# Output projections in four column quarters, with expert weights loaded during them

## What is computed

```
layer 0:  z = [attention(8 heads x 64), HGRN2 recurrence(8 heads x 64)]    # 544 x 1024
          h = h + z @ w_out_ab                                            # output projection 0
          h = h + moe(rmsnorm(h))
layer 1:  bg, cg, hh = split(rmsnorm(h) @ w_in_c)                         # 3 x 1024 columns
          g = bg * conv3(cg * hh)                                         # short convolution
          h = h + g @ w_out_c                                             # output projection 1
          h = h + moe(rmsnorm(h))
moe:      each frame takes its best of 4 groups and in it its best 2 of 8 experts;
          out = sum over both of  gate * (silu(x @ w1[e]) * (x @ w3[e])) @ w2[e]
```

## Time and profile before

| | us |
|---|---|
| median of 3 runs (1251.95 to 1252.97) | 1252.25 |
| profiled execution | 1252.11 |
| its span | 1250.4 |
| TensorE busy in it | 1019.9 (82%) |
| VectorE busy | 437.0 (35%) |
| ScalarE busy | 276.9 (22%) |
| GpSimd busy | 197.7 (16%) |
| moved by DMA | 282.56 MB, mean 226 GB/s |

### The profile page before, as it was taken

One profiled execution on the slowest core, in us unless ns is written; L12 is line 12 of the kernel. 1 busy time (PEld: TensorE's weight loads), 2 busy tenths in 40 slices (PEclk: granted clock), 3 DMA queues, 4 the chain that ended last, 5 costly groups with the idle time before them and its releaser, 6 DMA issues.

```text
span 1250.4 us, 17904 instructions
## 1 busy us (share of the span) xinstructions
PE 1019.9 (82%) x7539; PEld 766.2 (61%) x7539; DVE 437.0 (35%) x894; ACT 276.9 (22%) x538; POOL 197.7 (16%) x139
## 2 busy tenths in 40 slices
PE   5989999879789569987788259999995699777781
PEld 4988999754467345544444159999874455444440
DVE  5333574547823511101100466545435211110114
ACT  4244322125501111111111331221112112111110
POOL 3343431004210012211111000000000122111110
PEclk9999999767889769998888669999997699888996
DMA  6322221404002989999998822233228899999975
GB/s 209 89 68 77 93 81 37 109 9 153 2 6 101 373 308 413 415 417 416 416 416 336 256 70 75 76 101 117 1 101 336 333 412 415 416 417 415 417 313 223
DMA packets 110686, 282.56 MB, mean 226 GB/s; under 512 B 22890, under 2 KB 61846, under 8 KB 94196
## 3 DMA queue, kind: packets, MB, share of 16 engines
q1 hardware_dynamic: 100884, 263.66, 56.3%
q0 software_dynamic: 9728, 17.85, 3.8%
HBM read 270.57 MB, written 27.02 MB: 238 GB/s over the span
## 4 chain that ended last, share of the span: by engine, by line
PE 59%; DMA 22%; DVE 8%; SPq 5%; ACT 2%; issue 2%; POOL 1%; DVEq 0%; POOLq 0%; ACTq 0%
DMA w<-in_w_dram 16%; PE banks L981 12%; PE banks L902 11%; PE banks L846 9%; PE banks L621 8%; PE banks L913 4%; SPq L377 3%; PE banks L620 3%; DMA wab<-in_w_in_ab_dram 2%; DVE XN L1235 1%; PE banks L596 1%; DMA yab<-y_rows 1%; PE banks L712 1%; SPq L380 1%; DMA xr<-x_rows,gidx 1%
## 5 line engine op out<-in xcount | busy, mean ns | idle before, releaser
L902 PE MATMUL banks<-w,xgT 128*64 128x256 f32 x2048 | 258.8, 412 | 66.5 <-DMA w<-in_w_dram 65.8
L902 PEld LDWEIGHTS banks<-w,xgT 128*64 128x64 f32 x2048 | 160.9, 150 | 173.2 <-DMA w<-in_w_dram 68.3
L1592 DVE TENSOR_TENSOR hh<-banks,sg 128x128 f32<-128x128 f32 x64 | 18.7, 292 | 406.6 <-ACT sg L1169 360.2
L549 POOL DMA_INDIRECT y_rows<-ys,yidx x64 | 63.6, 994 | 380.9 <-ACT ys L1177 369.7
L913 PE MATMUL banks<-w,hT 128*64 128x512 f32 x512 | 116.9, 598 | 0.0
L981 PE MATMUL banks<-xc_hi,wc_hi 128*128 128x272 f32 x384 | 111.6, 291 | 1.4 <-DVE xc_lo L1248 1.4
L981 PE MATMUL banks<-xc_hi,wc_lo 128*128 128x272 f32 x384 | 112.1, 292 | 0.0
L981 PE MATMUL banks<-xc_lo,wc_hi 128*128 128x272 f32 x384 | 111.4, 290 | 0.0
L545 POOL DMA_INDIRECT xr<-x_rows,gidx x32 | 33.4, 1045 | 401.3 <-DVE yidx L1575 376.5
L621 PE MATMUL banks<-wab_hi,xc_hi 128*128 128x256 f32 (+1 forms) x320 | 91.2, 286 | 0.7 <-POOL wab_lo L534 0.7
L621 PE MATMUL banks<-wab_hi,xp_lo 128*128 128x256 f32 (+1 forms) x320 | 90.1, 282 | 0.0
(11 more groups left out here) (265 smaller groups left out, 1694.9 us busy)
## 6 DMA issues: line engine op xcount, KB each, us to landing
w<-in_w_dram SPq DMA_DIRECT2D x192, 1024.0 KB
wab<-in_w_in_ab_dram SPq DMA_DIRECT2D x13, 1024.0 KB, 5.1
wc<-in_w_in_c_dram SPq DMA_DIRECT2D x24, 512.0 KB, 5.9
yab<-y_rows SPq DMA_DIRECT2D x16, 512.0 KB, 7.1
wo<-in_w_out_ab_dram SPq DMA_DIRECT2D x2, 2048.0 KB, 11.3
x_rows<-XN SPq DMA_DIRECT2D x8, 512.0 KB, 20.2
woc<-in_w_out_c_dram SPq DMA_DIRECT2D x2, 2048.0 KB, 8.4
H<-in_x_prompt_dram SPq DMA_DIRECT2D x4, 512.0 KB, 8.4
```

The source lines that it names most:

```text
L549: pool.indirect_dma_start(y_dram[l][:, :], bass.IndirectOffsetOnAxis(ap=index.bitcast(U32), axis=0), ys[i][:, :], None, bounds_check=4 * T ...
L902: last = pe.matmul(bank[hb][64 * f:64 * f + 64, 0:2 * P].rearrange("p (w j) -> p w j", w=2), xgT[i][:, k, 64 * ab:64 * ab + 64], w13[s][:, ...
```

## The change

The output columns are done in four quarters of 256 (`OQ = 4`, `OW = 256`), so in 20 tiles, and the weights are loaded and split by quarters of 1 MB into three buffers; quarter 2 takes the buffer of quarter 0 when quarter 0 has been used. GpSimd splits only quarter 0 of layer 0. Quarters 1 to 3 are cast on ScalarE (`out_hi`) and subtracted on VectorE (`out_lo`) between the additions, behind tiles 1, 7 and 11; in layer 1 quarter 0 is split as the first half was. The attention's small tiles move into the expert slots' memory and the projection's operands out of it, so that slots 0 to 3 come free earlier: in layer 0 the first of them is loaded when zA is split, the next at the end of quarter 0, two more at the end of quarter 2; in layer 1 slot 0 is loaded before the convolution's last step, slot 1 at its end, 2 and 3 at the end of quarter 2. The normalized rows of the experts' input get a tile of their own, XF, and XT lies at the old place of XN. The slot order of layer 1 is now 0 to 5. Two waits of ScalarE (for output DMAs and for z_lo) are gone.

```diff
-SLOTS = [2, 3, 0, 1, 4, 5]
+SLOTS = [[2, 3, 0, 1, 4, 5], [0, 1, 2, 3, 4, 5]]
+OQ = 4
+OW = D // OQ
...
+        XF = at("XF", 152, [P, NC, D])
+        XT = at("XT", 132, [P, KT, T])
...
+        OUT_W = [[(RING + 32, RING + 40), (152, 160), (RING + 32, RING + 40), (172, 180)],
+                 [(RING + 65, RING + 73), (152, 160), (RING + 65, RING + 73), (189.5, 197.5)]]
...
+            def out_load(l, q):
+                w = (w_out_ab, w_out_c)[l]
+                sp.dma_start(wo[l][q][:], w[0, :, q * OW:(q + 1) * OW].rearrange("(k p) n -> p k n", p=P)).then_inc(out_arrived(l, q)[0], 16)
+            out_load(0, 0)
...
+            sp.wait_ge(s_ok, NC * NH)
+            out_load(0, 1)
             sp.wait_ge(rb_mm, NC)
             router_load(0)
+            sp.wait_ge(zA_ok, NC)
+            sp.wait_ge(out_dma, 16 * 8)
+            first_load(0, 0)
+            out_load(0, 3)
             sp.wait_ge(op_mm, NC)
-            first_load(0, 2)
-            sp.wait_ge(op_mm, 2 * NC)
-            for j in (0, 1, 3):
+            out_load(0, 2)
+            first_load(0, 1)
+            sp.wait_ge(op_mm, 3 * NC)
+            for j in (2, 3):
                 first_load(0, j)
...
-            for s in range(2):
-                pool.wait_ge(wo_in[s], 16)
-                if s == 1:
-                    pool.wait_ge(s_ok, NC * NH)
-                split([wo[s][:]], [wo_hi[s][:]], [wo_lo[s][:]])
+            pool.wait_ge(wo_in[0], 16)
+            split([wo[0][0][:]], [wo_hi[0][0][:]], [wo_lo[0][0][:]])
...
-                for i in range(2 * NC):
+                for i in range(OQ * NC):
...
-                            last = pe.matmul(bank[i % 4][0:ROWS[c], :], z(a, k)[:, c * P:c * P + ROWS[c]], w(b, k, s),
+                            last = pe.matmul(bank[i % 4][0:ROWS[c], 0:OW], z(a, k)[:, c * P:c * P + ROWS[c]], w(b, k, s),
...
+            def out_hi(l, q):
+                act.wait_ge(*out_arrived(l, q))
+                act.activation(wo_hi[l][q][:], wo[l][q][:], ACT.Copy).then_inc(w_hi, 1)
...
+            def out_lo(l, q):
+                dve.wait_ge(w_hi, 15 + OQ * l + q)
+                dve.tensor_tensor(wo_lo[l][q][:], wo[l][q][:], wo_hi[l][q][:].bitcast(F32), ALU.subtract).then_inc(w_lo, 1)
...
+                    if i in (1, 7, 11):
+                        out_lo(n, (1, 7, 11).index(i) + 1)
-                    if s == 1:
-                        dve.wait_ge(op_add, 2 * NC * n + i + 1)
+                    if s == OQ - 1:
+                        dve.wait_ge(op_add, OQ * NC * n + i + 1)
```

More of the change, by code:

```diff
@@ L249, in hmoe_step @@
         zAh_ok = sem("zAh_ok"); zA_ok = sem("zA_ok")
-        wo_in = [sem(f"wo_in{s}") for s in range(2)]
+        wo_in = [sem(f"wo_in{s}") for s in range(3)]
         op_mm = sem("op_mm"); op_add = sem("op_add")
@@ L272, in hmoe_step @@
         lbm_ok = sem("lbm_ok"); lbe_ok = sem("lbe_ok")
-        woc_in = [sem(f"woc_in{s}") for s in range(2)]
         NXT = 2 * NC
@@ L289, in fetched, with out_arrived @@
         def fetched(l, e):
-            s = SLOTS[e % 6]
-            return l * len([j for j in range(NE) if SLOTS[j % 6] == s]) + e // 6 + 1
+            s = SLOTS[l][e % 6]
+            return l * len([j for j in range(NE) if SLOTS[0][j % 6] == s]) + e // 6 + 1
+        def out_arrived(l, q):
+            return wo_in[(0, 1, 0, 2)[q]], 16 * ((2 * l + q // 2 + 1) if q % 2 == 0 else l + 1)
         def freed(unit, b):
@@ L1148, in _ @@
                     act.activation(kcT[:], bank[7][:, :].rearrange("p (m t) -> p m t", m=4), ACT.Copy).then_inc(kc_ok, 1)
+            def out_hi(l, q):
+                act.wait_ge(*out_arrived(l, q))
+                act.activation(wo_hi[l][q][:], wo[l][q][:], ACT.Copy).then_inc(w_hi, 1)
             def mixture(l):
+                if l == 0:
+                    act.wait_ge(w_lo, 15)
+                for q in range(1, OQ):
+                    out_hi(l, q)
                 squares(2 * l + 1)
```

118 lines of the change are left out of this document (53 added, 65 removed).

## The result

| | us |
|---|---|
| changed kernel, median of 12 runs (1252.58 to 1263.27) | 1258.36 |
| kernel before, median of 12 runs beside it | 1252.10 |
| ratio after to before, 95% interval | 1.0047 (1.0031 to 1.0063) |
| profiled execution of the changed kernel, its span | 1252.58, 1250.9 |

The profiled execution is the shortest of its twelve.

The account below looks back on a forecast made before the run. It took TensorE, VectorE's router steps and a gather to bound the stages before the experts, weight transfers the expert phases. Layer 0's -13.1 and layer 1's +4.9 made -8.2 from 1252.25, so 1244 us, range 1235 to 1252.

Parts of the forecast that it names:

- The lock: End of layer 0's attention: without GpSimd's second-half split locking VectorE out, the projection starts earlier, -10.1 us.
- The first quarter's split: Layer 0's attention: GpSimd still splits this quarter, VectorE goes first, dg ends later, +1.8 us, bounds 0 and +5.
- Clock: Layer 0's projection: without the ten idle us ahead of it the clock stays at 2.4 GHz, -2.9 us.
- Columns: Output projections: 480 matmuls of 256 columns replace 240 of 512, +1.0 us in each layer.
- Norms: End of each projection: additions come every 2.8 us, VectorE's norms fall behind, +1.5 us a layer, bounds 0.5 and 3.
- Gather: Before the first expert: the gather finds an almost empty queue and takes 4.3 us, -4.4 in layer 0, -2.6 in layer 1.
- The early slots shorten nothing: Expert phases: the seventh expert loads only after the first is computed, so a slot filled earlier saves nothing by itself.
- The rival's 1207: Expert phases: early slots shorten them by three experts of 7.6 us per layer, 45 us in all; chance 5%.
- The third quarter of layer 1: Layer 1's projection: this load, queued behind the tails, is split at 919.3 but needed at 914.4, +5 us.
- the tails cost the upper bound: Layer 1's projection: the quarter's signal waits for the tails, stall and clock add 9 us, so 1253; chance 10%.
- the tails cost nothing: Layer 1's projection: engines take the tails' small packets beside the large ones, so 1239 us; chance 20%.

Follow-up runs that it names:

- e4: Kernel before, with GpSimd's split of the second weight half waiting for the attention's end; 1244.04 us, ratio 0.9924.
- e10: Kernel before, with that split waiting for the attention's end and layer 1's tails written as 32 rows of 512 bytes; 1246.47 us, ratio 0.9923.
- e11: Changed kernel with tails as rows and the first quarter's split moved from GpSimd to ScalarE and VectorE; 1243.24 us, ratio 0.9906.
- e5: Changed kernel, layer 1's tail DMAs issued behind quarter 2 and after quarter 3's cast, in an idle stretch; 1244.11 us, ratio 0.9916.
- e8: Changed kernel, tails transposed into 32 rows of 512 bytes and issued behind quarter 2; 1243.33 us, ratio 0.9905.
- e3: Changed kernel, layer 1's four tail DMAs issued on GpSimd's queue instead of SP's at the same point; 1258.28 us, ratio 1.0040.
- e6: Changed kernel, tails still ahead of quarter 2, but quarter 3 and slot 1 loaded behind it; 1252.35 us, ratio 0.9991.
- e1: Changed kernel, layer 1's four tail DMAs issued just behind quarter 2's load instead of ahead; 1246.00 us, ratio 0.9951.
- e2: Changed kernel, layer 1's four tail DMAs issued behind slots 4 and 5 in the expert phase; 1253.91 us, ratio 1.0020.
- e9: The changed kernel run again, nothing altered; 1260.23 us, ratio 1.0053 to the kernel before.
- e13: Changed kernel with sixteen unused matmuls ahead of TensorE's wait for layer 1's last expert's weights; 1257.31 us, ratio 1.0041.
- e14: Changed kernel with tails as rows, plus sixteen unused matmuls ahead of layer 1's last expert; 1241.60 us, ratio 0.9908.

## Why the prediction was wrong, step by step

- **The lock (-10.1): right.** 9.85 in e4. In the changed kernel too `zA_lo` is 0.67 and `dg` 0.41. Its projection starts 52.7 us behind `zB_lo`'s start, before 61.6: -8.9, where the two terms together said -8.3. The other 2.6 of its 11.5 us came before `zB_lo`.
- **The first quarter's split (+1.8): right at its place.** Counted from `zB_lo`'s start `dg` ends 8.86 us later, before 6.95: +1.9. VectorE went first again. At the projection's start 0.2 to 1.1 us of it is left (51.9 to 52.7 us behind `zB_lo` in the kernels with the change, 51.7 in e4 and e10; e11 left out). The rows of the changed kernel:

```profile
284.63 3.39 DVE L1489 TENSOR_TENSOR zB_lo<-zB,zB_hi 128x2176 fp32r<-128x2176 f32 x1
289.06 4.43 DVE L1462 TENSOR_TENSOR dg<-ident,rinv 128x1024 f32<-128x1024 f32 x1
```

- **Clock (-2.9): wrong.** The clock was low behind the attention without the idle time too (0.52 in e4). I had read a cause into one pair of rows. **Columns (+1.0): right;** 384 matmuls in the 45 us from 349 to 394 are 117.2 ns each, +0.7 for 480.
- **Norms (+1.5): right in layer 1.** Columns and norms together +2.6 (last norm 64.4 us behind the start in e5, 61.8 in e4), forecast +2.5. In layer 0 the last norm comes 2.0 us later than before, counted from the start, instead of 0.4 earlier: the clock term.
- **A cost that I had not:** in layer 0 the router's stretch from the last norm to the gather is 1.6 us longer than before (31.3 for 29.7), and in e5 3.1, with 7.0 us for the logits that took 4.09; the granted clock there was 0.50 in e5 and 0.96 before.
- **Gather (-4.4 and -2.6): right, a little small in layer 1:** -4.45 and -3.56.
- **The early slots shorten nothing: right within a us or two.** From layer 1's first expert to the end 262.9 us, before 263.7; from layer 0's to the convolution 282.3, before 284.1. (The rival's 1207 is 45 us under 1252, not under the forecast; on top of the forecast it would be 1199. And the window 456 to 460 lies four to eight us behind the gather's landing, not five to nine. Neither bears on the result.)
- **The third quarter of layer 1 (+5, bounds 0 and +14): the step that failed.** Measured from the projection's start the last norm comes 19.2 us later than before. Less 2.6 for columns and norms that is 16.6: 13.8 idle and 2.8 of clock. It is the rival "the tails cost the upper bound", and beyond it. That rival had 10%.

Layer 1's sum then closes: 16.6 + 2.6 - 3.6 = +15.6 to its first expert (15.7 before rounding), where I had +4.9. With -14.4 up to its projection and -0.8 in the expert phase that is +0.5, from 1252.1 to the 1252.6 of the profiled execution; 2.6 of the -14.4 are not the change's, and without that luck this execution too would have been some 3 us slower than the kernel before.

That e5 and e8 come to 1244.1 and 1243.3 does not save the forecast of 1244. Its sum without a stall is 1239; they lie 4 to 5 us above it, by layer 0's clock (2.9), the router (3.1 in e5) and the last expert's low clock (4.3 in e5, 268.0 for 263.7), less some smaller gains.

Three errors made the step too small:

1. I costed the tails by engine time, 7.4 us, as if packets and loads took turns. The figure itself varies (10 us in e5), and it is not the measure: in e3 the tails took 0.4 us of it (1.2% of 32 us) and cost as much. What they cost is slow packets of the load behind them (e6, 893 to 900 us).
2. I took SP's issue as free, since it was 0.39 to 0.58 us a DMA in the earlier trace rows. There the queue in front was empty. Behind 5 MB of loads the same four DMAs held SP for 14.36 us, and the quarter went out 5.7 us late. My own account had listed what is queued ahead, but asked only when it lands.
3. I took the landing of 10.6 to 18.0 us in the earlier trace rows for a lag of the tails' own signals, and let it count in full only for the bound. The transfers that were issued near the tails and waited for landed 5 to 16 us late (11.88, 15.41, 16.58, 17.12, 18.00, 22.68 us). The rule of the Trainium skill (DMA: Bandwidth & Descriptors, Queues, rings and completion order) that the prediction cited there, a completion lands only after every earlier write of its engine, is not what made the changed kernel late. There the bytes themselves came late: 0.73 of the quarter's 1.05 MB moved after 906, the last before 909, and it landed at 909.36. Only in e1 does the signal lag: from 895 to 901 us nothing but small packets moves, and the quarter lands at 900.56.

```profile
DMA packets 2022, 0.01 MB, mean 1 GB/s; under 512 B 2022, under 2 KB 2022, under 8 KB 2022
```

In e1, though, the tails were issued behind the quarter, so they are not earlier writes of its queue.

By these runs the upper bound was the likeliest value, and the side on which I put the chance (20% for "the tails cost nothing") was the wrong one.

## What to carry to other kernels

Before a load that is waited for is put near small stores, count the single numbers that are written, on all queues, and not the bytes or their engine time: here 16 KB in 4-byte stores cost about 15 us. On another queue they cost the same (e3); behind the load they still cost 5 us of its landing, though the time fell by 12 (e1); ahead of a gather they cost 14 us of it (e2). An idle stretch, or a transpose into rows, took the cost away. An issue time read behind an empty queue doesn't hold behind a full one. And when a change has many parts, the part that takes a VectorE operation out from under a GpSimd instruction may be most of its gain: here one exchanged wait (0.9924) was worth what the whole change was worth without its stall, within the intervals. Before two profiles are compared by absolute times, find a place ahead of the change and count from there: here it had moved by up to 5 us.

## What the runs showed of the hardware

- Four stores of 4096 single numbers, 4160 packets on SP's queue, take the 16 transfer engines 10 us at 2 to 4 GB/s (e5; 7.4 us in the kernel before), and hold up a 1 MB load by 5 to 16 us whether it is issued before them (e1, 11.88 us), 7 us after them (e6, 16.58), or on another queue than theirs (e3, 22.68), against 6.4 us without them (e2).
- The load's packets of 1 KB take 0.17 us each in the seven us after the last small packet (e6) and 0.32 in the changed kernel, against 0.05 a few us later. On GpSimd's queue the same stores are 128 packets and 1.2% of 32 us, and the delay is no smaller (e3).
- SP was held 14.36 us (e9 16.50, e13 12.68) by issuing those four DMAs behind 5 MB, and 2.26 us behind one quarter (e6) or an idle queue (e5).
- A subtraction of 128x2048 on GpSimd took 6.57 us with VectorE's `zB_lo` and `dg` beside it and 4.60 elsewhere (`wab_lo`), and the `dg` took 4.43 us, for 1.22 without it (e11).
- The granted clock was 0.52 from 337 to 343 us of e4, behind twelve us in which TensorE was busy for 9.45. It stayed at 1.00 when sixteen small matmuls (3.84 us) filled a wait of some 4 us (e14), which without them had ended at 0.53 (e8).
